# Cached pages laid over 64 partitions in 4 KB runs instead of 128 partitions in 2 KB runs

## What is computed

```
def fox_sample(q, k, v, logf, k_past, v_past, logf_past):
    d_new = lax.cumsum(logf, axis=1).transpose(0, 2, 1)
    rev = (lax.cumsum(logf_past, axis=1, reverse=True) - logf_past).transpose(0, 2, 1)
    sp = jnp.einsum('bqhd,bkhd->bhqk', q, k_past) * scale
    sp = sp + d_new[:, :, :, None] + rev[:, :, None, :]
    ...
    p = jax.nn.softmax(jnp.concatenate([sp, sn], axis=-1), axis=-1)
    out = (jnp.einsum('bhqk,bkhd->bqhd', p[..., :n_past], v_past)
           + jnp.einsum('bhqk,bkhd->bqhd', p[..., n_past:], v))

k_past = cache_k[l][page_table].reshape(db, past_len, N_HEADS, HEAD_DIM)
v_past = cache_v[l][page_table].reshape(db, past_len, N_HEADS, HEAD_DIM)
lf_past = cache_logf[l][page_table].reshape(db, past_len, N_HEADS)
```

## Time and profile before

| | us |
|---|---|
| median of three timed executions | 2016.37 |
| the profiled execution | 2018.6 |
| its span, first to last instruction | 2016.9 |
| PE busy | 1876.5 (93%) |
| DVE busy | 861.9 (43%) |
| ACT busy | 440.3 (22%) |
| POOL busy | 249.4 (12%) |
| DMA, share of 16 engines: q1 / q0 | 50.8% / 12.8% |

### The profile page before, as it was taken

One profiled execution on the slowest core, in us unless ns is written; L12 is line 12 of the kernel. 1 busy time (PEld: TensorE's weight loads), 2 busy tenths in 40 slices (PEclk: granted clock), 3 DMA queues, 4 the chain that ended last, 5 costly groups with the idle time before them and its releaser, 6 DMA issues.

```text
span 2016.9 us, 33708 instructions
## 1 busy us (share of the span) xinstructions
PE 1876.5 (93%) x12473; PEld 1121.2 (56%) x12473; DVE 861.9 (43%) x1921; ACT 440.3 (22%) x1017; POOL 249.4 (12%) x381
## 2 busy tenths in 40 slices
PE   6999998888999999999999998987999999999994
PEld 4677655555488868888874487444333333333331
DVE  5644467777656523333344647245111111111115
ACT  3111124444301011101110305131222222212213
POOL 0203333333100000000000000000111111111110
PEclk9999999999999999999999999996999999999997
DMA  7859999999911140210121205344999999999966
GB/s 255 277 169 343 354 337 364 352 339 347 331 63 65 44 154 11 63 53 11 55 74 63 87 1 183 121 171 177 372 381 382 374 373 376 371 372 374 371 222 264
DMA packets 208164, 458.57 MB, mean 227 GB/s; under 512 B 18721, under 2 KB 47418, under 8 KB 207618
## 3 DMA queue, kind: packets, MB, share of 16 engines
q1 hardware_dynamic: 177554, 365.30, 50.8%
q0 software_dynamic: 30448, 91.13, 12.8%
HBM read 432.44 MB, written 32.17 MB: 230 GB/s over the span
## 4 chain that ended last, share of the span: by engine, by line
PE 82%; DVE 6%; ACT 4%; DMA 4%; issue 3%; DVEq 1%; SPq 0%; ACTq 0%; POOLq 0%; POOL 0%
PE ps L1338 20%; PE ps L1691 11%; PE ps L1722 6%; PE ps L1167 6%; PE ps L1403 6%; PE ps L1702 6%; PE ps L1432 5%; PE ps L1731 3%; PE ps L1182 3%; PE ps L1544 2%; PE ps L1290 2%; PE ps L1270 2%; PE ps L1148 1%; DVE kt L2230 1%; DMA vpage<-in_cache_v 1%
## 5 line engine op out<-in xcount | busy, mean ns | idle before, releaser
L1691 PE MATMUL ps<-gu,xgT 128*64 128x512 f32 x1024 | 228.7, 599 | 0.6 <-ACT xgT L2046 0.6
L1338 PE MATMUL ps<-xnT,ring 128*128 128x264 f32 x768 | 184.5, 392 | 3.2 <-ACT xnT L741 1.9
L2230 DVE STREAM_TRANSPOSE kt<-kraw 128x1024 f32<-128x1024 f32 x128 | 151.1, 1219 | 34.5 <-DMA kraw<-in_cache_k 25.3
L1338 PEld LDWEIGHTS ps<-xnT,ring 128*128 128x128 f32 x768 | 147.8, 193 | 30.5 <-ACT xnT L741 2.2
L876 POOL DMA_DIRECT2D vpage<-in_cache_v x228 | 122.4, 537 | 291.6 <-PE ps L1290 233.6
L3053 DVE TENSOR_TENSOR sig_a<-ps,sig_a 128x256 f32<-128x256 f32 x32 | 13.6, 425 | 322.9 <-ACT sig_a L2050 322.9
L1691 PEld LDWEIGHTS ps<-gu,xgT 128*64 128x64 f32 x1024 | 71.1, 138 | 133.0 <-issue 130.2
L1722 PE MATMUL ps<-wd,hidT_a 128*64 128x512 f32 x512 | 116.9, 598 | 20.2 <-ACT hidT_a L2056 11.2
L1702 PE MATMUL ps<-gu,xgT 128*32 128x512 f32 x1024 | 115.8, 592 | 0.0
L1167 PE MATMUL ps<-xnT,early 128*128 128x352 f32 x320 | 101.2, 472 | 4.4 <-DVE xnT L2174 4.4
L1167 PEld LDWEIGHTS ps<-xnT,early 128*128 128x128 f32 x320 | 60.6, 194 | 38.2 <-issue 8.7
(11 more groups left out here) (482 smaller groups left out, 2945.9 us busy)
## 6 DMA issues: line engine op xcount, KB each, us to landing
kraw<-in_cache_k SPq DMA_DIRECT2D x256, 256.0 KB, 5.3
wd<-in_w_expert_down SPq DMA_DIRECT2D x31, 2048.0 KB, 21.5
gu<-in_w_expert_gate SPq DMA_DIRECT2D x30, 2048.0 KB, 20.3
gu<-in_w_expert_up SPq DMA_DIRECT2D x30, 2048.0 KB, 25.1
vpage<-in_cache_v POOLq DMA_DIRECT2D x228, 256.0 KB, 5.8
ring<-in_w_in SPq DMA_DIRECT2D x12, 1024.0 KB, 8.1
yy<-y_d SPq DMA_DIRECT2D x16, 512.0 KB, 10.4
early<-in_w_in SPq DMA_DIRECT2D x6, 1024.0 KB, 11.7
```

Source lines behind the costliest of these rows:

```text
L1338: last = nc.tensor.matmul(bank(R.bank(name, f, q))[:, 0:QT], weight[:, k], src[:, k, cols], start=k == 0, stop=k == HK - 1)
L1691: last = nc.tensor.matmul(bank(0)[h * BA:(h + 1) * BA, :].rearrange("p (x n) -> p x n", x=2), src[:, k, 0:BA], weight[:, k, :, h * DE // 2 ...
L2230: nc.vector.transpose(kt[n % 2].rearrange("p c e s -> p (c e s)")[:, x * 1024:(x + 1) * 1024], kraw[n % 2].rearrange("p c d -> p (c d)")[: ...
```

## The change

A page now lies in 64 neighbouring partitions, with two successive tokens (4 KB, contiguous in memory) in each, for keys and values. Pages 0 and 2 of a unit go to partitions 0 to 63, pages 1 and 3 to partitions 64 to 127; pages 0 and 1 share one 4 KB stretch of the buffer, pages 2 and 3 the other.

```diff
+        def page_rows(place, p):
+            return place[p % 2 * 64:p % 2 * 64 + 64, p // 2 * 2:p // 2 * 2 + 2, :]
+
+        def page_pairs(cache, page):
+            return cache[ds(page, 1)].rearrange("a (s j) d -> (a s) j d", j=2)
...
-                eng.dma_start(vpage[value_place(n)][:, p, :], t["cache_v"][ds(page, 1)].rearrange("a s d -> (a s) d")
+                eng.dma_start(page_rows(vpage[value_place(n)], p), page_pairs(t["cache_v"], page)
...
-            eng.dma_start(kraw[n % 2][:, p, :], t["cache_k"][ds(page, 1)].rearrange("a s d -> (a s) d")
-                          ).then_inc(k_in[n % 2], 16)
+            eng.dma_start(page_rows(kraw[n % 2], p), page_pairs(t["cache_k"], page)).then_inc(k_in[n % 2], 16)
```

```diff
-    g, j = r // PAGES, r % PAGES
+    g, j = r // (PAGES // 2), r % (PAGES // 2)
...
-                sp.dma_start(pgi, t["pages"].rearrange("a (g p) -> p (a g)", g=2)).then_inc(tables_in, 16)
+                sp.dma_start(pgi, t["pages"].rearrange("a (p g) -> p (a g)", g=2)).then_inc(tables_in, 16)
...
-                    sp.wait_ge(rev_stored, 16 * 8)
+                    sp.wait_ge(rev_stored, 16 * 4)
...
-                        nc.tensor.matmul(bank(R.bank("later", g))[:, 0:H], consts[:, C_PAGES:C_PAGES + P], ptot[:, g, :],
-                                         start=True, stop=True).then_inc(R.full, 1)
+                        for x in range(2):
+                            last = nc.tensor.matmul(bank(R.bank("later", g))[:, 0:H], consts[:, C_PAGES:C_PAGES + P],
+                                                    ptot[:, x, :], start=x == 0, stop=x == 1 and g == 1)
+                        if g == 0:
+                            last = nc.tensor.matmul(bank(R.bank("later", g))[:, 0:H], ident, ptot[:, 1, :],
+                                                    start=False, stop=True)
+                        last.then_inc(R.full, 1)
...
-                nc.vector.tensor_tensor(after[:, g], after[:, g], bank(R.bank("later", g))[:, 0:H].unsqueeze(2)
-                                        .to_broadcast([P, H, PAGE]), ALU.add)
+                for odd in range(2):
+                    nc.vector.tensor_tensor(paired[:, g, :, :, odd, :].rearrange("p x h s -> p h x s"),
+                                            after[:, g].rearrange("p h (x s o) -> p h x s o", o=2, s=32)[:, :, :, :, odd],
+                                            bank(R.bank("later", g))[:, 0:H].unsqueeze(2).unsqueeze(3)
+                                            .to_broadcast([P, H, 2, 32]), ALU.add)
...
-            for half in range(2):
-                for g in range(4):
-                    pool.dma_start(rev_d[g].rearrange("h (x s) -> x h s", s=32)[half * P:(half + 1) * P],
-                                   after[:, half, :, g * 32:(g + 1) * 32]).then_inc(rev_stored, 16)
-            pool.wait_ge(rev_stored, 16 * 8)
+            for g in range(4):
+                pool.dma_start(rev_d[g].rearrange("h (x s) -> x h s", s=64),
+                               paired[:, g // 2, g % 2].rearrange("p h o s -> p h (o s)")).then_inc(rev_stored, 16)
```

More of the change, by code:

```diff
@@ L243, in build_program @@
         after = at("after", [P, 2, H, PAGE], w + 5 * 4096)
+        paired = at("paired", [P, 2, 2, H, 2, 32], w)
         ptot = at("ptot", [P, 2, H], w + 7 * 4096)
```

## The result

Four executions of the changed kernel took 2153.62 to 2170.30 us, median 2164.02; four of the kernel before 2015.75 to 2018.55, median 2016.48. The ratio is 1.0739, with a 95% interval of 1.0713 to 1.0764: slower by 148 us. The direction and the mechanism of the forecast held, its size did not: 108 us were expected from the page transfers, and what follows the stage of the pages starts 148.6 us later. The profiled execution took 2168.5 us, its span is 2166.8.

The account below looks back on a forecast made before the run. Between 150 and 535 us PE, then DMA, was taken to bound the kernel. Page transfers +108, longer runs -3 and forget rows +1 on the profiled 2018.6 gave 2124.6, or 2122 us against the median; range 2001 to 2225.

Parts of the forecast that it names:

- What bounds the kernel: 150 to 535 us: PE first, DMA later; slower transfers paid almost in full, faster ones give at most PE's idle 37.4 us.
- Longer runs, 0 to 18, value 3: Page loads: 4 KB runs in place of 2 KB save 0 to 18 us, taken as 3.
- Fewer partitions, +108: Page stage: loads into 64 neighbouring partitions move slower, 493 us in place of 385, +108 us.
- the mean of 263 GB/s: Page loads: half the bytes at 212 GB/s (both streams in one half), half at 346 (opposite halves); pages take 451 us.
- the other 14.6 MB: Page stage: forget rows, weights, stored keys and values, taken to stay at 346 GB/s, 42 us.
- Rival A: Page stage: keys and values wait at one half together, 212 GB/s throughout, +216, 2230 us; chance 0.14.
- Rival B: Page stage: few partitions don't hold loads and longer runs pay, 2008 us, at best 1980; chance 0.31.
- C: Page stage: a wash, the runs return a small partition loss or PE hides it, 2014 to 2020 us; chance 0.12.
- D: Page loads: the runs stay 2 KB; it was given nothing.
- Forget rows, +1: Forget rows: fewer, larger stores and a removed wait give nothing; extra DVE and PE work, total +1 us.
- The first 150 us, at most +5: 100 to 150 us: keys alone need 175 GB/s, no cost, up to 5 us if weight loads push keys back.
- The signs: Page stage: DMA share near 1, about 263 GB/s, page landing 8 us, end near 640 us, waits near 100, later work unchanged.

Follow-up runs that it names:

- the two mixed runs: Changed kernel with only keys, or only values, in 64 neighbouring partitions, the other in 128 as before: 2121.27 and 2135.89 us, against 2012.03 for the kernel before.

## Why the prediction was right in kind and short by 42 us

*What bounds the kernel.* "Whatever slows the transfers is paid almost in full": right, the lower rate makes 145 of the 148.6 us. "Whatever speeds them gives back at most the 37.4 us": true only as a bound; 27 MB less gave 4 us, and in every other partition, where q1 moved 23.0 GB/s for one engine in place of 22.0, nothing came back. The premise read from the earlier trace rows alone, that PE's idle time is time lost to pages, falls; the list of waits would have shown it beforehand. Nor did the chain agree: the earlier trace rows shows its longest landings, but from 150 to 560 us only 10.8% of it, 44 us, lies in vpage and kraw. In the changed kernel it is 51.9% from 150 to 760 us.

*Longer runs, 0 to 18, value 3.* The change of layout without the loss is 0.35% slower than before, and undoing the runs within the change made no difference that can be told. The value is 0; the earlier trace rows had said so.

*Fewer partitions, +108.* The mechanism held, the term was too small, in two places. First and surely, the mean of 263 GB/s: its lower term was 212, measured 200 to 205; its upper term, opposite halves without loss at 346, is 285 measured with both queues moving. With 285 in its place and all else as forecast the mean is 243, the pages take 487 us and the sum is +145, what was found. So exact a fit is luck: the lower term was off too, and so was the rate of the other bytes, both towards more time. With 200 below as well the mean is 235, close to the 231 to 234 of such pages alone, and the sum +161; the kernel did better, 251 for all its bytes. Second, the other 14.6 MB were left at 346 GB/s, as though wide transfers beside narrow ones were free; the two mixed runs and the landing of `early` show they are not. If all bytes are given the measured 251, the pages take 118.5 / 0.251 = 472 us in place of 451 (+21) and the rest 58 in place of 42 (+16), and the 37 with the forecast 108 are the 145 of the stage. That is bookkeeping with a rate that was read from the stage itself; how the 37 us divide between the two places is not shown.

*Rival A* (212 throughout, 2230) was right that opposite halves cost each other something, 285 rather than 346, and wrong that they end up at one half throughout. The truth lies between it and the forecast.

*Rival B* (faster, 2008, at best 1980) had two premises, both refuted: steady loads are held, and PE's waits for pages were 8.7 us, not 37.4. *C* is what the layout does in every other partition (+0.35%). *D* didn't happen: q1's packets fell by 15045.

*Forget rows, +1.* Measured alone +2.4, 0 to 5: right within what can be told. The values started 15 us earlier (57.55 for 72.51), without use.

*The first 150 us, at most +5.* Right: PE loses 1.9 us between 50 and 100 us and nothing from 100 to 150, and its first products with values start at 159.8 us in place of 157.8, though the DMA share there rose from 0.54 to 0.82.

*The signs.* Share near 1 with a lower rate, both queues alike, everything behind unchanged: as predicted. A page lands in 10.3 to 10.6 us, not 8, the stage ends near 680, not 640: the same mis-sized term. The waits were to grow "to a sum near 100"; they are 158.1 and 86.4. They grew by 212 us together for a loss of 148, so a good part of this waiting happens on both at once or off the path.

*Sum.* The span grew by 149.9 us where 106 was forecast. Of the 43.9 between, 37 is the rate (both places above together), 3 the longer runs that gave nothing, 2.6 what the rounded ends of the stage (150 to 535, 150 to 680) leave once the forecast 1 for forget rows is taken off, and 1.3 lies behind the stage. The median is 4.5 us under the profiled execution, where 2.2 was used. 43.9 less 2.3 is the distance from 2122 to 2164.

*Open.* Why the pages with 11% of wide bytes between them move at 251 GB/s and alone at 231; by a plain mean, 118.5 / 0.231 + 14.6 / 0.346 = 555 us, 240 GB/s are expected. Whether the lower granted clock (0.86 to 0.90) adds anything in the stage was not tried: the value products became longer, 694 for 625 ns, while over half of the chain (51.9% from 150 to 760 us) lies in landings of pages. And why the pages in every other partition are 0.35% slower, 0.12% of it from the forget rows, though their waits for keys fell from 25.3 to 17.1 us, is not settled. The only version that was faster than the kernel before is the one that leaves loads out.

## What to carry to other kernels

Choose partitions for a transfer by which they are, not by how many: 64 in the lower or upper half move at half rate in both directions, while every other one, or 32 to 95, move at the full rate. One such stream slowed the other beside it (16.9 and 17.2 GB/s for one engine in place of 22.4 and 22.0), so don't leave the rest of a stage at its old rate. And a DMA share near 1 doesn't prove that faster transfers would help: the list of waits names what releases the idle engine, and here it came much nearer to the gain (8.7 us, measured 4) than PE's idle time did (37.4). The loss from slower transfers has no such bound.

## What the runs showed of the hardware

Loads into partitions 0 to 63 and stores out of them are held alike, 202 to 212 GB/s against 395 to 409 for all partitions. Two queues in opposite halves gave 285 and 306 GB/s while both moved, 80 to 100 more than one half gives (200 to 205) and still far from the full rate. With both queues in 32 to 95 it was 393, so the number of queues isn't what costs. Packets of 2 KB and of 4 KB on q1 gave the same stage. A landing time of 5.7 us became 10.3 to 10.6 for the same 256 KB, and a row of `neg_d` spread over all partitions beside the pages (512 KB) took 16.9 us, before 9.3.
